# A two-layer diffusion trunk on one core: the norm of the second token block moves into the FFN's block, beside the first halves of six products

## The chip, the core and the metric

One core of a Trainium2 chip runs the whole program in one launch. The metric is the device time in microseconds. Engines by their names in the profile: PE (TensorE), DVE (VectorE), ACT (ScalarE), POOL (GpSimd), SP (SyncE, which here issues all the DMAs of the part in question).

## What is computed

Two layers work on 128 context tokens and 1024 latent tokens (1152 in all, 1024 features, fp32). The part around the change is the second half of each layer:

```
x = x + g1 * (y @ w_out)                       # y: output of the mixer
h = rms(x, norm_w[l, 1]) * (1 + sc2) + sh2     # mean square over the 1024 features of a token
u = dwconv(h @ w_up, conv_w, conv_b)           # 5632 columns, taps of 3 over the tokens
x = x + g2 * ((silu(a) * b) @ w_down)          # a, b: the halves of u
```

A product of fp32 quality is three matmuls on values split into a high and a low part (`split_matmul`, L89 to L91).

## The kernel before

Everything is kept transposed: features on the 128 partitions, tokens along the free axis, so x is the tile `x_t` of 8 rows of 1152 tokens. `P` is 128, `KT` 8, `KH` 4, `HALF` 576 tokens, `SIDE` and `SUB` 288. A *token block* b is the b-th quarter of each half of the tokens: 288 tokens of the left half and 288 of the right ("sides"). Each scope is a `Block` in which every engine has a program of its own; engines meet at its end. Semaphores order the work inside.

**`out_norm`** computes 16 output tiles v = 0 to 15 (`OUT_TILES`): 8 feature rows for token block 0, then the same 8 for block 1. For a tile PE does 2 sides x 8 rows x 3 matmuls of 288 columns. DVE adds the result to `x_t` (`add`, L634), ACT and DVE split the weights two tiles ahead into high and low (`split_w`, L495 and L625), ACT squares the new row (`square`, L505), and DVE adds the square to the running sum (`pile`, L644). PE waits for the low weights of tile v and for the add of tile v - 3. After 8 rows PE sums over the partitions with a matrix of ones (`total`, L590), and ACT takes ln and exp (`root`, L510, L513), which gives the inverse root mean square. Then come four norm steps q for the block, each of two feature rows (q and q + 4): DVE scales (`scale`, L653), ACT applies gain and shift (`shift`, L521), DVE forms four differences (`differences`, L661 to L666), and seven operands are split into high (ACT, L532 and L537) and low (DVE, L671 and L679) in `acts`. These are the seven activation operands of a Strassen form: the tokens' halves and the features' halves are the 2 x 2 blocks.

The steps of token block 0 run beside the tiles v = 8 to 15, placed by the dicts `begun`, `turned_in` and `ended` (a step every two tiles, from v = 8). Those of block 1 (q = 4 to 7) run after the last tile, in a loop at the end of the ACT and DVE programs. SP spills x to DRAM (`spill`, L463): block 0 after `load_w(11)`, block 1 at the end, and waits for both.

**`strassen_ffn`** then does the FFN. It has 22 steps t over pairs of weight tiles, each of 7 products i of 2 x 4 x 3 matmuls of 288 columns (168 a step). POOL forms four sums of weight quarters (L912, L913, L915, L919; the third of them makes product 1's operand), ACT makes `w_hi` (L938), DVE `w_lo` (L1049), PE multiplies, and ACT (`copy_m1`, L944) and DVE (`recombine`, L1068) read the seven results. On DVE the low part of the next step's operand i stands between the reads: lo(t+1, 0), read 0, lo(t+1, 1), read 1, lo(t+1, 2), and so on. The results use four pairs of PSUM banks in turn. The memory of `x_t` is reused (`take`): for `u`, `conv`, `m1`, the sums, the last quarter of the odd steps' weights and the taps `cw`. Step 0's weights are loaded in `out_norm` already (`ahead`). Ahead of its first instruction ACT, like DVE, waits for `cw`.

Of the kernel before, what the change touches and what calls it, by code (L numbers as in the profile page):

```python
# [377 lines left out]
def out_norm(nc, tag, l, d, x_t, y_tok, ident, x_from, x_to, ones, eps, mods, gains, acts, raw, w_first, ahead):  # L378
# [7 lines left out]
    with Scope(nc, tag) as s:  # L386
# [7 lines left out]
        x_in, spilled = [s.sem(f"x_in{k}") for k in range(KT)], s.sem("spilled")  # L394
# [53 lines left out]
        begun = {KT: 0, KT + 2: 1, KT + 4: 2, KT + 6: 3}  # L448
        turned_in = {KT + 1: 0, KT + 3: 1, KT + 5: 2, KT + 7: 3}
        ended = {KT + 2: 0, KT + 4: 1, KT + 6: 2, KT + 7: 3}  # L450

        with nc.Block() as block:
            @block.sync
            def _(sp):
# [25 lines left out]
                spill(1)  # L480
                sp.wait_ge(spilled, 16 * 2 * KT)
# [6 lines left out]
            def _(act):  # L488
# [72 lines left out]
                root(1)  # L561
                shift(KH)
                for q in range(KH, N_STEPS):
                    high_plain(q)
                    if q + 1 < N_STEPS:
                        shift(q + 1)
                    high_diff(q)

            @block.tensor
            def _(pe):  # L570
# [45 lines left out]
                pe.wait_ge(inverted, 1)  # L616
                total(1)

            @block.vector
            def _(dve):  # L620
# [17 lines left out]
                def pile(v_):  # L638
                    b, k = divmod(v_, KT)
                    if k:  # L640
                        dve.wait_ge(squared, v_ + 1)
                        if k >= 2:
                            dve.wait_ge(piled, (KT - 1) * b + k - 1)
                        dve.tensor_tensor(inv[:, b, :], inv[:, b, :], sq[:, k % 2, :], ALU.add).then_inc(piled, 1)  # L644
# [51 lines left out]
                for v_ in range(OUT_TILES):  # L696
# [3 lines left out]
                    if v_ in ended and v_ not in turned_in:  # L700
                        low_diff(ended[v_])
# [3 lines left out]
                    if v_ in ended and v_ in turned_in:  # L705
                        low_diff(ended[v_])
                    if v_ in begun:
                        scale(begun[v_])
                scale(KH)
                for q in range(KH, N_STEPS):  # L710
                    differences(q)
                    if q + 1 < N_STEPS:
                        scale(q + 1)
                    low_plain(q)
                    low_diff(q)


G_SLOTS = 4

# [24 lines left out]
def strassen_ffn(nc, tag, l, d, x_t, mods, acts, raw, arrived, x_from, x_to):  # L744
# [5 lines left out]
    with Scope(nc, tag) as s:  # L750
        odd = s.sb("raw_odd", [P, 3, QW])
        w_hi, w_lo = s.sb("w_hi", [P, ACTS, QW], F32R), s.sb("w_lo", [P, ACTS, QW], F32R)
        ps = s.bank_pairs(4)
        cw_in = s.sem("cw_in")
        odd_in = [s.sem("odd_in0"), s.sem("odd_in1")]
# [18 lines left out]
        sums = [take(QW) for _ in range(4)]  # L774
        odd_last = take(QW)
        cw = take(FT * 2 * 4).rearrange("p (t h n) -> p t h n", h=2, n=4)
# [9 lines left out]
        def source(t, i):  # L786
            return sums[SUM_OF[i]] if i in SUM_OF else quarter(t, *RAW_OF[i])
# [4 lines left out]
        def halves(t, i):  # L792
            return pair_of(t, i)[:, :, 0:SUB]

# [34 lines left out]
        with nc.Block() as block:  # L829
            @block.sync  # L830
            def _(sp):
                sp.dma_start(cw, d["ffn_conv"][l]).then_inc(cw_in, 16)
# [48 lines left out]
                for n, (b, f, j, _) in enumerate(steps):  # L881
# [5 lines left out]
                    if n % FT == 10:  # L887
                        sp.wait_ge(g_stored, 16 * FT)
# [13 lines left out]
            def _(pool):  # L902
                Scope.clear_ended(pool)
                for t in range(FT):
                    (a1, a2), (b1, b2) = [[quarter(t, half, part) for part in range(2)] for half in range(2)]
                    for half in range(2):
# [2219 lines left out]
```

## Time and profile before

| | us |
|---|---|
| median of 3 runs | 3456.2 (3452.51 to 3477.64) |
| the profiled execution | 3463.67 |
| its span, first to last instruction | 3461.6 |
| PE busy | 3231.2 (93%) |
| DVE busy | 1865.5 (54%) |
| ACT busy | 1415.6 (41%) |
| POOL busy | 460.2 (13%) |
| granted clock of PE, mean | 0.958 |

All times of rows are of the profiled execution, in us from the span's start. Layer 0's `out_norm` ends and its FFN begins at about 910 us, layer 1's at about 2680 us. A row's start and duration can overlap the next row's by a pipeline's depth.

### The profile page before, as it was taken

What the parts mean: (1) busy time and instruction counts of PE and PEld (TensorE: products, weight loads), DVE (VectorE), ACT (ScalarE), POOL (GpSimd) and SP (SyncE); (2) the same over time, 40 slices, a digit from 0 to 9 for tenths busy, and PEclk for the clock granted to TensorE, in tenths of its full rate; (3) what the DMA queues carried; (4) which work ended last, traced back from release to release, by engine and by line L of the source; (5) the groups of instructions that cost most, each with busy time, mean ns of one, the idle gap of its engine ahead of it and who ended that gap; (6) DMA issues with size and microseconds to landing.
All of it is one profiled execution on the core that took longest, in us unless ns stands there. A gap on an engine that the chain in (4) does not pass through costs nothing. (4 is left out here: it accounts for less than half of the span.)

```text
span 3461.6 us, 57673 instructions
## 1 busy us (share of the span) xinstructions
PE 3231.2 (93%) x23164; PEld 2961.8 (86%) x23164; DVE 1865.5 (54%) x3213; ACT 1415.6 (41%) x2415; POOL 460.2 (13%) x370
## 2 busy tenths in 40 slices
PE   5999988889599999999799999999985999999998
PEld 3998755669599999999588997877775999999998
DVE  4321265455777777533523102677657777777432
ACT  4354115774533333422426213455546333333322
POOL 0000361000122222000000001111100322220000
PEclk7999999999799999999899998999988999999999
DMA  5115541014222221544634314222132222223643
GB/s 221 43 71 184 181 149 41 2 42 139 66 77 77 77 76 55 193 151 145 255 133 159 122 53 149 93 69 100 31 131 89 73 77 77 77 77 103 212 158 120
DMA packets 157512, 376.11 MB, mean 109 GB/s; under 512 B 23552, under 2 KB 92672, under 8 KB 149312
## 3 DMA queue, kind: packets, MB, share of 16 engines
q1 hardware_dynamic: 142176, 345.29, 29.3%
q0 software_dynamic: 4704, 17.70, 1.4%
q10 hardware_dynamic: 10368, 9.44, 0.8%
q8 instruction: 185, 3.03, 0.4%
q14 instruction: 79, 0.65, 0.1%
HBM read 292.03 MB, written 80.35 MB: 108 GB/s over the span
## 5 line engine op out<-in xcount | busy, mean ns | idle before, releaser
L89 PE MATMUL ffn__pair<-hf__acts,ffn__w_hi 128*128 128x288 f32 x2464 | 726.5, 295 | 66.7 <-DVE ffn__w_lo L1049 66.7
L91 PE MATMUL ffn__pair<-hf__acts,ffn__w_hi 128*128 128x288 f32 x2464 | 728.6, 296 | 0.0
L90 PE MATMUL ffn__pair<-hf__acts,ffn__w_lo 128*128 128x288 f32 x2464 | 727.0, 295 | 0.0
L89 PEld LDWEIGHTS ffn__pair<-hf__acts,ffn__w_hi 128*128 128x128 f32 x2464 | 463.8, 188 | 68.3 <-DVE ffn__w_lo L1049 68.3
L90 PEld LDWEIGHTS ffn__pair<-hf__acts,ffn__w_lo 128*128 128x128 f32 x2464 | 463.7, 188 | 0.0
L91 PEld LDWEIGHTS ffn__pair<-hf__acts,ffn__w_hi 128*128 128x128 f32 x2464 | 463.6, 188 | 0.0
L89 PE MATMUL ffn__pair<-hf__acts 128*128 128x384 f32 x1056 | 352.9, 334 | 2.9 <-issue 2.9
L91 PE MATMUL ffn__pair<-hf__acts 128*128 128x384 f32 x1056 | 352.7, 334 | 0.0
L90 PE MATMUL ffn__pair<-hf__acts 128*128 128x384 f32 x1056 | 352.7, 334 | 0.0
L1082 DVE SCALAR_TENSOR_TENSOR all__x_t<-all__x_t 128x127 f32<-128x127 f32 x352 | 271.1, 811 | 29.4 <-ACT all__x_t L951 29.3
L938 ACT ACTIVATE ffn__w_hi<-all__x_t 128x512 fp32r<-128x512 f32 x198 | 125.5, 635 | 380.3 <-PE ffn__pair L91 363.6
L1068 DVE TENSOR_TENSOR all__x_t<-ffn__pair,all__x_t 128x576 f32<-128x576 f32 x308 | 228.2, 753 | 87.5 <-PE ffn__pair L91 82.0
L89 PEld LDWEIGHTS ffn__pair<-hf__acts 128*128 128x128 f32 x1056 | 198.2, 188 | 3.3 <-issue 3.3
L90 PEld LDWEIGHTS ffn__pair<-hf__acts 128*128 128x128 f32 x1056 | 198.2, 188 | 0.0
L91 PEld LDWEIGHTS ffn__pair<-hf__acts 128*128 128x128 f32 x1056 | 198.2, 188 | 0.0
L1096 DVE TENSOR_TENSOR hf__acts<-all__raw,hf__acts 128x1024 fp32r<-128x1024 f32 x100 | 122.4, 1224 | 132.2 <-ACT hf__acts L966 132.0
L2869 DVE COPY_PREDICATED lin__att<-lin__mask,lin__pair 128x384 f32<-128x384 int16 x168 | 118.5, 705 | 113.2 <-PE lin__pair L2764 100.9
L2764 PEld LDWEIGHTS lin__pair<-lin__qz,lin__f 64*128 64x128 f32 x2016 | 142.1, 195 | 38.7 <-issue 35.0
L972 ACT ACTIVATE hf__acts<-ffn__raw_odd 128x384 fp32r<-128x384 f32 x132 | 68.4, 518 | 240.9 <-PE ffn__pair L91 217.9
L2764 PE MATMUL lin__pair<-lin__qz,lin__f 64*128 64x64 f32 x2016 | 165.4, 286 | 1.0 <-DVE lin__att L2869 1.0
L89 PE MATMUL out__bank<-hf__acts 128*128 128x288 f32 x512 | 153.5, 300 | 9.5 <-DVE hf__acts L625 8.6
L1049 DVE TENSOR_TENSOR ffn__w_lo<-all__x_t,ffn__w_hi 128x512 fp32r<-128x512 f32 x198 | 155.5, 786 | 8.7 <-ACT ffn__w_hi L938 8.7
(355 smaller groups left out, 6911.1 us busy)
## 6 DMA issues: line engine op xcount, KB each, us to landing
all__raw<-w_down SPq DMA_DIRECT2D x100, 512.0 KB, 3.7
ffn_g<-all__x_t SPq DMA_DIRECT2D x44, 576.0 KB, 3.2
ffn__raw_odd<-ffn_g SPq DMA_DIRECT2D x132, 192.0 KB, 3.7
all__raw<-w_up SPq DMA_DIRECT2D x44, 512.0 KB, 4.7
in__ada_w<-w_ada SPq DMA_DIRECT2D x16, 1024.0 KB, 5.2
n1a__ada_w<-w_ada SPq DMA_DIRECT2D x16, 1024.0 KB, 8.5
out__w_raw<-w_out SPq DMA_DIRECT2D x28, 512.0 KB, 3.6
all__raw<-w_t SPq DMA_DIRECT2D x27, 512.0 KB, 4.3
```

The lines of the kernel that those rows point to most:

```text
L89: pe.matmul(out, w_hi, v_lo, start=first, stop=False)
L90: pe.matmul(out, w_lo, v_hi, start=False, stop=False)
L91: return pe.matmul(out, w_hi, v_hi, start=False, stop=last)
L938: act.activation(w_hi[:, i, :], source(t, i), ACT.Copy).then_inc(hi_done, 1)
L972: act.activation(g_hi(n), g_raw(n), ACT.Copy).then_inc(g_hi_done, 1)
L1049: dve.tensor_tensor(w_lo[:, i, :], source(t, i), w_hi[:, i, :].bitcast(F32), ALU.subtract)\
L1068: dve.tensor_tensor(split2(out), halves(t, PRODUCT_OF[r]), split2(kept), ALU.add)\
L1082: dve.scalar_tensor_tensor(conv[half][:, o[0]:o[1]], u[half][:, i[0]:i[1]], cw[:, t, half, 2 * right:2 * right + 1], conv[half][:, o[0]:o[1]],
L1096: dve.tensor_tensor(lo, dn_raw(j), hi.bitcast(F32), ALU.subtract).then_inc(dn_lo_done, 1)
L2764: last = pe.matmul(scores[m % 2][:, h, c * half:(c + 1) * half], f[rows_of(h), n % 3, 2 + j, c * P:(c + 1) * P], qz[rows_of(h), n % 2, j, ...
L2869: dve.copy_predicated(out[:, :, :, late:late + size], msk.to_broadcast([P, 2, late_cols // size, size]), scores[m % 2][:, :, 0:late_cols]. ...
```

## The change

In `out_norm` the norm steps of token block 0 are placed closer (two steps in three tiles), and those of block 1, with PE's last `total`, the last `root` and `spill(1)`, are taken out. The last `pile` writes its sum into row 0 of block 0 of `x_t`, which has been spilled by then.

```diff
-        begun = {KT: 0, KT + 2: 1, KT + 4: 2, KT + 6: 3}
-        turned_in = {KT + 1: 0, KT + 3: 1, KT + 5: 2, KT + 7: 3}
-        ended = {KT + 2: 0, KT + 4: 1, KT + 6: 2, KT + 7: 3}
+        begun = {KT: 0, KT + 1: 1, KT + 3: 2, KT + 4: 3}
+        turned_in = {KT + 1: 0, KT + 2: 1, KT + 4: 2, KT + 5: 3}
+        ended = {KT + 2: 0, KT + 3: 1, KT + 5: 2, KT + 6: 3}
...
-                spill(1)
-                sp.wait_ge(spilled, 16 * 2 * KT)
...
+                        if v_ == OUT_TILES - 1:
+                            dve.wait_ge(spilled, 16 * KT)
+                            dve.wait_ge(scaled, 2 * KH)
+                            out = both(x_t[:, 0, :], 0)
```

In `strassen_ffn` the norm's work buffers lie in block 0 of `x_t`, and step 0 keeps its sums outside it (`sum_at`: in `odd` and in the place of one weight quarter). What reuses `x_t` waits for `room_free`: all 28 low parts of the norm and both spills. Weights of step 1 wait for step 0's low parts, because `odd` holds step 0's sums.

```diff
+FIRST_BANKS = ((0, 6), (1, 7), (2, 0), (3, 6), (4, 1), (5, 7), (2, 0))
+FREED_WITH = (5, 6, 6, 6, 0, 0, 0)
...
+        def room_free(eng):
+
+            eng.wait_ge(n_lo_done, ACTS * KH)
+            eng.wait_ge(spilled, 16 * 2 * KT)
+
+        def sum_at(t, n):
+            if t:
+                return later_sums[n]
+            return quarter(0, 1, 0) if n == 2 else odd[:, (0, 1, None, 2)[n], :]
...
+                for k in range(KT):
+                    into = x_from[:, k, :].rearrange("p (a n) -> p a n", a=2)[:, :, SIDE:2 * SIDE]
+                    sp.dma_start(into, both(k, 1)).then_inc(spilled, 16)
...
+                    else:
+                        sp.wait_ge(lo_done, ACTS)
...
+                            if t == 1 and part:
+                                room_free(sp)
...
+                    if t == 1:
+                        room_free(pool)
                     pool.tensor_tensor(sums[0], b1, b2, ALU.add).then_inc(summed, 1)
+                    if t == 0:
+                        pool.wait_ge(summed, 1)
...
-                act.wait_ge(cw_in, 16)
...
-                for i in range(ACTS - 1):
+                for i in range(3):
                     hi_up(0, i)
+                root()
+                hi_up(0, 3)
+                shift(0)
+                for q in range(KH):
+                    high_plain(q)
+                    if q + 1 < KH:
+                        shift(q + 1)
+                    high_diff(q)
+                    if q < 3:
+                        hi_up(0, 4 + q)
```

`copy_m1` and `recombine` of step 0 wait for `room_free` and read each side with an instruction of its own. `cw` has memory of its own, and its wait stands at its first use. PE begins with the `total` of block 1, does the first sides (block 0) of products 0 to 5, then the second sides of products 0 and 1 row by row as the norm delivers them, then the rest:

```diff
+                for i in range(6):
+                    pe.wait_ge(lo_done, i + 1)
+                    for k in range(KH):
+                        first_half(i, 0, k)
+                pe.wait_ge(n_logged, 2)
+                for k in range(KH):
+                    pe.wait_ge(n_lo_done, ACTS * (k + 1))
+                    for i in range(2):
+                        op = first_half(i, 1, k)
+                        if k == KH - 1:
+                            op.then_inc(mm, 1)
+                for i in range(2, 6):
+                    if i < 4:
+                        pe.wait_ge(m1_copied, 1)
+                    else:
+                        pe.wait_ge(recombined, LAST_READ[1])
+                    for k in range(KH):
+                        op = first_half(i, 1, k)
+                    op.then_inc(mm, 1)
+                pe.wait_ge(lo_done, 7)
+                pe.wait_ge(recombined, LAST_READ[2])
+                for side in range(2):
+                    for k in range(KH):
+                        op = first_half(6, side, k)
+                op.then_inc(mm, 1)
+                for t in range(1, FT):
...
-                for i in range(ACTS - 1):
+                for i in range(3):
                     lo_up(0, i)
+                scale(0)
+                lo_up(0, 3)
+                for q in range(KH):
+                    differences(q)
+                    if q + 1 < KH:
+                        scale(q + 1)
+                    low_norm(q)
+                    if q < 3:
+                        lo_up(0, 4 + q)
```

Products 0 to 3 of step 1 wait for later reads of step 0 than before, since the banks of step 0 are laid out otherwise: product 0 for the sixth read (`FREED_WITH[0]` is 5, `LAST_READ[5]` is 6), products 1 to 3 for the seventh. `root`, `shift`, `scale`, `differences` and the splits are the same instructions as in `out_norm`, for latent tokens alone. The same change holds in both layers.

## Rows read from the trace of the kernel before

**Rows 1.** Busy time by stretch: PE, PEld, DVE, ACT, POOL, clock, DMA share, GB/s

```profile
840.00:860.00 20.00, 20.00 (x154) 20.00 (x154) 17.07 (x33) 13.99 (x27) 0.00 (x0) 1.00 0.26 79
880.00:900.00 20.00, 1.47 (x4) 0.50 (x2) 16.04 (x38) 15.66 (x31) 0.00 (x0) 0.50 0.24 83
900.00:920.00 20.00, 5.54 (x26) 5.54 (x27) 13.61 (x29) 9.62 (x21) 5.47 (x4) 0.52 0.19 58
```

**Rows 2.** Waits in both layers' seams: engine, line, releaser, total us, times, longest

```profile
PE ffn__pair L89 <- DVE ffn__w_lo L1049: 33.0, 1, 33.0
...
PE ffn__pair L89 <- DVE ffn__w_lo L1049: 33.7, 1, 33.7
```

**Rows 3.** Timeline of PE, layer 0, then layer 1: start us, us, instruction

```profile
879.22 2.26 PE L590 MATMUL out__bank<-out__inv,all__ones 128*128 128x288 f32 x4 [3.15 <-DVE out__inv L644]
...
914.46 0.61 PE L89 MATMUL ffn__pair<-hf__acts,ffn__w_hi 128*128 128x288 f32 x1 [32.98 <-DVE ffn__w_lo L1049]
...
2684.29 0.61 PE L89 MATMUL ffn__pair<-hf__acts,ffn__w_hi 128*128 128x288 f32 x1 [33.68 <-DVE ffn__w_lo L1049]
```

**Rows 4.** Timeline of DVE, last output tiles of layer 0

```profile
853.79 1.23 DVE L625 TENSOR_TENSOR hf__acts<-out__w_raw,hf__acts 128x1024 fp32r<-128x1024 f32 x1 [1.68 <-ACT hf__acts L495]
...
876.18 0.94 DVE L634 SCALAR_TENSOR_TENSOR all__x_t<-out__bank,all__mods,all__x_t 128x288 f32<-128x288 f32 x2
...
878.31 0.76 DVE L644 TENSOR_TENSOR out__inv<-out__inv,out__sq 128x576 f32<-128x576 f32 x1 [1.19 <-ACT out__sq L505]
...
881.69 1.55 DVE L679 TENSOR_TENSOR hf__acts<-out__diff,hf__acts 128x288 fp32r<-128x288 f32 x4
```

**Rows 5.** Waits, 780 to 1000 us: DVE for ACT's weight split

```profile
DVE hf__acts L625 <- ACT hf__acts L495: 5.0, 3, 1.7
```

**Rows 6.** Timeline of ACT: the root of the second block, layer 0

```profile
881.16 1.28 ACT L510 ACT_TABLE_LOAD   x1
...
884.66 0.68 ACT L513 ACTIVATE out__inv<-out__inv 128x576 f32<-128x576 f32 x1
```

**Rows 7.** Timeline of DVE: norm of the second block, layer 0

```profile
887.82 0.46 DVE L661 TENSOR_TENSOR out__diff<-out__v 128x288 f32<-128x288 f32 x1 [1.02 <-ACT out__v L521]
...
893.87 0.46 DVE L661 TENSOR_TENSOR out__diff<-out__v 128x288 f32<-128x288 f32 x1
...
908.68 1.55 DVE L679 TENSOR_TENSOR hf__acts<-out__diff,hf__acts 128x288 fp32r<-128x288 f32 x4
```

**Rows 8.** Timelines of SP, ACT, POOL: start of the FFN block, layer 0

```profile
910.51 0.34 SPq L832 DMA_DIRECT2D all__x_t<-ffn_conv  x1
...
912.39 0.63 ACT L938 ACTIVATE ffn__w_hi<-all__raw 128x512 fp32r<-128x512 f32 x1 [4.26 <-DMA all__x_t<-ffn_conv]
...
912.59 1.26 POOL L912 TENSOR_TENSOR all__x_t<-all__raw 128x512 f32<-128x512 f32 x1 [350.36 <-issue]
...
916.81 0.63 ACT L938 ACTIVATE ffn__w_hi<-all__x_t 128x512 fp32r<-128x512 f32 x1 [3.79 <-POOL all__x_t L915]
...
917.35 0.61 ACT L938 ACTIVATE ffn__w_hi<-all__raw 128x512 fp32r<-128x512 f32 x1
```

**Rows 9.** Timelines of DVE and POOL: FFN steps 0 and 1, layer 1

```profile
2688.45 0.68 DVE L1049 TENSOR_TENSOR ffn__w_lo<-all__raw,ffn__w_hi 128x512 fp32r<-128x512 f32 x1
...
2690.56 1.53 POOL L912 TENSOR_TENSOR all__x_t<-ffn__raw_odd,all__x_t 128x512 f32<-128x512 f32 x1 [2.58 <-DVE ffn__w_lo L1049]
...
2693.75 1.74 POOL L915 TENSOR_TENSOR all__x_t<-all__x_t,ffn__raw_odd 128x512 f32<-128x512 f32 x1
...
2696.20 1.28 DVE L1049 TENSOR_TENSOR ffn__w_lo<-all__x_t,ffn__w_hi 128x512 fp32r<-128x512 f32 x1 [1.19 <-ACT ffn__w_hi L938]
```

**Rows 10.** DMA issues, 910 to 918 us: KB each, us to landing

```profile
all__x_t<-w_up SPq DMA_DIRECT2D x1, 256.0 KB, 4.4
```

**Rows 11.** Timeline of ACT, both layers: copy after the first product of step 1

```profile
942.32 0.65 ACT L944 ACTIVATE all__x_t<-ffn__pair 128x576 f32<-128x576 f32 x1 [2.49 <-PE ffn__pair L91]
...
2711.38 0.65 ACT L944 ACTIVATE all__x_t<-ffn__pair 128x576 f32<-128x576 f32 x1 [2.48 <-PE ffn__pair L91]
```

More of the change, by code:

```diff
@@ L375, with out_norm @@
 N_STEPS = 2 * KH
[L378 removed]
+def out_norm(nc, tag, l, d, x_t, y_tok, ident, x_from, x_to, ones, eps, mods, gains, acts, raw, w_first, spilled, ahead):
     by_token = y_tok is not None
@@ L699, in _ @@
                     pile(v_)
-                    if v_ in ended and v_ not in turned_in:
+                    if v_ in ended:
                         low_diff(ended[v_])
@@ L773, in strassen_ffn, with both, h, diff @@
         m1, u2, u3 = take(HALF), take(HALF), take(HALF)
-        sums = [take(QW) for _ in range(4)]
+        later_sums = [take(QW) for _ in range(4)]
         odd_last = take(QW)
-        cw = take(FT * 2 * 4).rearrange("p (t h n) -> p t h n", h=2, n=4)
+        def both(row, b):
+            return x_t[:, row, :].rearrange("p (a n) -> p a n", a=2)[:, :, b * SIDE:(b + 1) * SIDE]
+        inv = both(0, 0)
+        def h(q, half):
+            return both(1 + 2 * (q % 2) + half, 0)
+        def diff(n):
+            return both(5 + n // 2, 0)[:, n % 2, :]
+        def plain(q, i):
+            half, side = {Q11: (0, 0), Q21: (1, 0), Q22: (1, 1)}[i]
+            return h(q, half)[:, side, :]
+        def home(q, i, low):
+            return acts[:, i, low, q, SIDE:2 * SIDE]
+        def room_free(eng):
[5 more added lines that the diff above has]
+            return quarter(0, 1, 0) if n == 2 else odd[:, (0, 1, None, 2)[n], :]
         def quarter(t, half, part):
@@ L786, in source @@
         def source(t, i):
-            return sums[SUM_OF[i]] if i in SUM_OF else quarter(t, *RAW_OF[i])
+            return sum_at(t, SUM_OF[i]) if i in SUM_OF else quarter(t, *RAW_OF[i])
         def pair_of(t, i):
@@ L905, in _ @@
                     (a1, a2), (b1, b2) = [[quarter(t, half, part) for part in range(2)] for half in range(2)]
+                    sums = [sum_at(t, n) for n in range(4)]
                     for half in range(2):
@@ L972, in hi_down, with root, shift, high_plain @@
                     act.activation(g_hi(n), g_raw(n), ACT.Copy).then_inc(g_hi_done, 1)
-                for i in range(ACTS - 1):
-                    hi_up(0, i)
+                def root():
+                    act.wait_ge(n_summed, 1)
+                    for side in range(2):
+                        act.activation(inv[:, side, :], ps[3][:, side, 0:SUB], ACT.Ln, bias=eps[:, 0:1], scale=1.0 / D)\
+                            .then_inc(n_logged, 1)
+                    act.wait_ge(n_logged, 2)
+                    act.activation(inv, inv, ACT.Exp, scale=-0.5).then_inc(n_inverted, 1)
+                def shift(q):
+                    for half in range(2):
+                        k = q + KH * half
+                        act.wait_ge(n_scaled, 2 * q + half + 1)
+                        act.activation(h(q, half), h(q, half), ACT.Identity, bias=mod(mods, l, SH2, k, 1),
+                                       scale=gains[:, l, 1, k, 1:2]).then_inc(n_shifted, 1)
+                def high_plain(q):
+                    act.wait_ge(n_shifted, 2 * q + 2)
+                    for i in (Q11, Q21, Q22):
+                        act.activation(home(q, i, 0), plain(q, i), ACT.Copy).then_inc(n_hi_done, 1)
+                def high_diff(q):
+                    for n, i in enumerate((T1, T3, T2, T4)):
+                        act.wait_ge(n_diffed, 4 * q + n + 1)
+                        act.activation(home(q, i, 0), diff(n), ACT.Copy).then_inc(n_hi_done, 1)
+                for i in range(3):
+                    hi_up(0, i)
+                root()
[8 more added lines that the diff above has]
+                        hi_up(0, 4 + q)
                 for t in range(FT):
-                    hi_up(t, 6)
+                    if t:
+                        hi_up(t, 6)
                     copy_m1(t)
```

113 lines of the change are left out of this document (77 added, 36 removed).

## The prediction

> **What bounds the kernel now.** I read the page first: PE is busy in 93% of the span, so only stretches where PE stands still, or runs at the lower clock, can give time back. The busy time by stretch shows them: from 840 to 860 us PE works without a gap (154 matmuls in 20 us, 0.130 us each), from 880 to 900 only four matmuls run and the clock is at 0.50, and from 900 to 920 26 run at 0.52 [rows 1]. The waits name the gap: in each layer PE waits once for the first `w_lo` of the FFN, 33.0 and 33.7 us [rows 2]. So there are two seams, one a layer; I work one out on layer 0. PE ends the last product of `out_norm` at 876.07 (the `total` starts at 879.22 after 3.15 us of idle time), and starts the first FFN matmul at 914.46 [rows 3]. Two seams of 38.4 us hold 77 us, 2.2% of the time. That is the most that could be had, and the question is how far it shrinks.
>
> Inside the seam DVE sets the pace: it goes from one operation to the next through the four norm steps (first difference at 887.82, last low part ends at 908.68 + 1.55 = 910.23 [rows 7]), with ACT beside it. Then come 4.2 us of block change, the wait of ACT for `cw` (issued at 910.51, ACT starts at 912.39 [rows 8]) and one split. After that PE has 168 matmuls for step 0. The mark I carry through is the end of the first product of step 1, which ACT's copy follows at once: 942.3 in layer 0, 2711.4 in layer 1 [rows 11]. From there on PE is continuous before, and I find nothing in the change that touches it later. PE's own sum agrees: 914.46 + 192 x 0.1315 = 939.7 (0.1315 is the spacing of neighbouring rows), 2.2 us for the low clock at the start (26 matmuls took 5.5 us in place of 3.4 [rows 1]), and the pipeline's depth.
>
> **The change, step by step, in layer 0.** The tail of the old chain is shortened by overlap, but three pieces ahead of it get longer.
>
> *Closer steps in `out_norm`.* Before, DVE ends its work on token block 0 and the last tile at 881.69 + 1.55 = 883.24, and the last `pile` ended at 878.31 + 0.76 = 879.07, with eleven operations of step 3 behind it [rows 4]. A tile takes PE 48 x 0.1315 = 6.3 us. DVE needs for a tile 0.94 (add) + 1.2 (split) + 0.75 (pile) = 2.9 us [rows 4] and for a norm step some 6.0 us (the period of the steps in the seam [rows 7], the same operations). One step in two tiles is 5.9 us a tile, just under 6.3. Two steps in three tiles is 6.9, over it. So DVE falls behind from tile 9 on. Now all of step 3 stands ahead of the last `pile`, so by the sum of the work that one ends at 883.24 at the earliest with the old gaps. There is one more gap: after each `scale` ACT's shift stands ahead of its weight split, and DVE waits for it, 1.68 us, three times before, 5.0 us in all [rows 5], four times now, less some overlap at the end. I take 1.5 us: the block ends at 884.7, 5.6 us later than the old `pile`. On the way the low weights of tiles 13 to 15 come late, and PE stands about 3.6 us there. Bounds: no slip (0), and 7.5 us.
>
> *The way to the inverse.* Before, the `total` followed the `pile` and the exp ended at 884.66 + 0.68 = 885.34, 6.3 us after the `pile` [rows 6]. Now ACT does `hi_up(0, 1)` and `hi_up(0, 2)` first, and the first of them waits for POOL's third sum. From the block's end to POOL's first sum: 912.59 - 910.23 = 2.4 us; to ACT's second split, released by that third sum, 916.81 - 912.59 = 4.2 us; the two splits 1.1 us [rows 8]; then the root, 4.2 us from the table load on [rows 6]. Together 11.8 us, 5.5 more than before. The inverse is ready at 896.5. Nothing covers this: DVE has only three weight splits to do meanwhile. The new order inside POOL (second sum behind the first) adds under 0.1.
>
> *The norm itself.* Before 910.23 - 885.34 = 24.9 us [rows 6, 7]. In it now stand `lo_up(0, 4)`, (0, 5), (0, 6), 0.6 us each in a queue that has no gap (0.68 less the overlap with the next [rows 9]); `lo_up(0, 3)` falls into the 1.0 us in which DVE waited for the first shift [rows 7]. So 26.7 us, and the last low part ends at 923.2 = N, 13 us later than before. ACT's four extra splits fit into its pauses. The spill now runs beside this and is long done; before it was hidden too.
>
> *The tail.* Before: 942.3 - 910.23 = 32.1 us. After N PE has left 6 + 48 + 24 = 78 matmuls of step 0, 10.3 us, in place of 22.1. But step 1's first product has to wait for the sixth read of step 0, and that stands in DVE's queue behind `lo_up(1, 1)`, which waits for POOL's third sum of step 1, which waits for `room_free` and for the last quarter of its weights. That quarter's DMA is issued only at N. Its landing took 4.4 us beside three other loads [rows 10]; the small `cw` 1.9 us [rows 8]; I take 3.0 for 256 KB alone. Three sums of POOL: 2693.75 + 1.74 - 2690.56 = 4.9 us beside DVE's splits, three times 1.26 = 3.8 alone [rows 8, 9]; I take 4.4. ACT's split 0.65. Then on DVE `lo_up(1, 1)` 0.7 to 1.3 [rows 9], five reads at 0.85 (two instructions of 288 columns; an `add` of that size takes 0.94 [rows 4]), three more splits at 0.6: 7.1 us with the splits. Sum 3.0 + 4.4 + 0.65 + 7.1 + waits 0.4 = 15.6 us. PE itself could be there at N + 0.9 + 0.9 (copy of `m1`) + the rest of the 78 + 2.2 for the clock, about N + 14, so DVE decides. The product takes 3.3 us more: N + 18.9 = 942.1. Bounds for the tail: 2.4 us less (everything uncontended), 4.7 more.
>
> The Trainium skill, SBUF — State Buffer, Who interferes with whom, says that a DVE instruction with two SBUF inputs contends with a GpSimd instruction that reads SBUF, while one with at most one SBUF input does not. Rows 9 fit the first half. By the second half the reads, which take one input from PSUM, would leave POOL alone, the three sums would take 3.8 us, and each seam would be 0.6 us shorter than I say.
>
> **Sum.** Layer 0: 942.1 against 942.3, -0.2 us. Layer 1 repeats layer 0 with an offset of 1769.83 (2684.29 against 914.46 [rows 3]), but its clock rose earlier and its mark stood 0.8 us earlier in that frame, so there it is +0.6 us. Together +0.4 on the profiled execution's 3463.67 (its span is 3461.6, and it lies 7.5 above the median of 3456.2). Carried to the median: 3456.5 us. In parts, a seam: + 5.6 + 5.5 + 1.8 - 13.2.
>
> **Rivals.** *Slip absent, faster.* DVE keeps up in `out_norm`, because its gaps close instead of opening. For it: DVE has 1.7 us gaps there [rows 5]. Against: those gaps are waits for ACT, and they recur with each step. Price 5.6 a seam: 3445 us. *Nothing given back, faster.* The steps come in time and the root is not delayed either: 12 to 13 us a seam, 3431 us. Against: the chain of program orders above; it needs two things not to happen. *The clock, slower.* PE works in short bursts during the norm, and the granted clock was 0.50 to 0.52 around the gap [rows 1], the lower of the two levels (1.2 GHz); it rose only within the continuous run behind it. In the new tail PE has pauses (the copy of `m1`, the second read, the sixth read). If it stayed low there, 78 matmuls at 0.24 us each (288 columns at 1.2 GHz) take 18.7 us, plus 1.8 of waits: PE is at N + 20.5 and not at 15.6, and the next product runs low too, + 2.6. That is +7.5 a seam: 3471 us, slower than before. It decides once more than some 30 of the 78 run low. Against: before it rose within about 20 matmuls. The Trainium skill, TensorE: Matmul & The Clock Gate, The HAM clock gate, says "the default state is throttled, and activity releases the throttle"; by that the bursts would not help, and only the run after N would, which is this rival's first half. That the first sides are not done early at all can be left out: they wait for weights alone, and the last of those, `lo_up(0, 5)`, stands behind the second norm step.
>
> **How the numbers follow.** Forecast (a wash, within 4 us) 0.6; slip absent 0.17; nothing given back 0.05; clock 0.18. The bounds of the parts are -8 and +8 a seam, so -16 and +16. The median of few runs moves by some us as well (3452.5 to 3477.6 before). Range 3441 to 3471. One per cent, about what a measurement of this kernel can tell from no change, is 34.6 us: no rival reaches it. Faster by more: 0.02; within: 0.95; slower: 0.03, for a wait that I have not seen.
>
> **What would show it.** Right: `pile` of tile 15 ends 5 to 6 us later; PE waits for `w_lo` in tiles 13 to 15; exp ends 11 to 12 us behind it; the last low part of the norm near 923; the sixth read sets the start of step 1 near N + 15.6; copy of `m1` of step 1 at about 942 and 2712. Wrong: a continuous PE through tile 15, a clock at 0.5 beyond N + 6, or a gap of PE in steps 1 to 3.

## The result: 60 us longer in its first four executions, outside the place of the change

The changed kernel took 3526.2 us (median of 4 executions, 3523.4 to 3529.6), the kernel before 3466.2 (4 executions, 3452.5 to 3477.6; three of them are the three of the table above). That is 60 us more, and 70 more than the forecast of 3456.5, whose range went up to 3471. The ratio is 1.0175, 95% interval 1.0127 to 1.0223. Ratios leave out executions that are over 1.5% above the fastest of the same kernel, called long below, but here all four of the changed kernel are long by the measure of its later sets, so none was left out.

The page of the changed kernel, its profiled execution (3529.56 us):

```profile
span 3527.8 us, 57691 instructions
...
PE 3324.6 (94%) x23164; PEld 3033.8 (86%) x23164; DVE 1860.6 (53%) x3227; ACT 1417.3 (40%) x2417; POOL 460.2 (13%) x370
...
PEclk8999989999899999999899995589989899999999
```

PE has the same 23164 matmuls, and 93.4 us more of busy time than the 3231.2 before. The granted clock has two digits of 5 in a row. A digit is a fortieth of the span, 88 us: these two are 2117 to 2293 us. The change acts at two places, near 890 and near 2720 us, and neither is there. The row of the kernel before has an 8 and a 9 in that place:

```profile
PEclk7999999999799999999899998999988999999999
```

The busy time by stretch says it with numbers. It is the linear scans of layer 1, code that the change doesn't touch (PE busy and its matmuls, clock, DMA share, GB/s; PE's rows alone). Before, then after:

```profile
2150.00:2200.00 50.00, 50.00 (x490) 1.00 0.26 94
2200.00:2250.00 50.00, 49.76 (x483) 1.00 0.32 112
2250.00:2300.00 50.00, 49.63 (x467) 1.00 0.19 62
```

```profile
2150.00:2200.00 50.00, 50.00 (x272) 0.50 0.18 64
2200.00:2250.00 50.00, 50.00 (x269) 0.50 0.09 32
2250.00:2300.00 50.00, 50.00 (x270) 0.50 0.17 58
2300.00:2350.00 50.00, 49.76 (x394) 0.83 0.24 83
```

PE is busy in 49.6 us or more of every 50 in both, and issues little more than half as many matmuls in the second. Single rows of PE's timeline in that stage show why, first before, then after:

```profile
2144.82 0.50 PE L2721 MATMUL lin__bank<-lin__spans,lin__g_hi 128*128 128x512 f32 x1
2145.16 0.39 PE L2722 MATMUL lin__bank<-lin__spans,lin__g_lo 128*128 128x512 f32 x1
2145.49 0.89 PE L2764 MATMUL lin__pair<-lin__qz,lin__f 64*128 64x64 f32 x12
```

```profile
2143.21 0.79 PE L2878 MATMUL lin__bank<-lin__spans,lin__g_hi 128*128 128x512 f32 x1
2143.80 0.63 PE L2879 MATMUL lin__bank<-lin__spans,lin__g_lo 128*128 128x512 f32 x1
...
2145.84 1.55 PE L2921 MATMUL lin__pair<-lin__qz,lin__f 64*128 64x64 f32 x12
```

At full clock (2.4 GHz) twelve small matmuls take 0.89 us, at the lower level (1.2 GHz) 1.55. In the profile before, PE was at the lower level for 17.1 us from 2127.5 on, and rose at 2144.6. In the profile after it was there from 2129.7 on, for 187.7 us. Until the one rises the two executions run 2.3 to 2.4 us apart, matmul by matmul. These are the longest stretches near the start of the scans; each profile has others too, in the first 11 us and at the end of the scans (36.9 us before, 6.0 after). All together PE spends 65.6 us of the scans at the lower level before and 205.2 after. Below, *the low stretch* is the longest one near the start.

So the extra time splits as follows, each part from PE's timelines. *Out* is the first product of `out_norm` (the row `out__bank<-hf__acts`), *down* the first matmul of the FFN's down product (its first row with 384 columns).

| us | before | after | difference |
|---|---|---|---|
| up to *out*, layer 0 | 767.1 | 772.8 | +5.7 |
| *out* to *down*, layer 0 (the change) | 640.81 | 638.96 | -1.85 |
| first to last matmul of layer 1's scans | 416.3 | 480.8 | +64.5 |
| *out* to *down*, layer 1 (the change) | 638.89 | 637.72 | -1.17 |

The 5.7 us arise before anything of the change has run; PE's time at the lower level there is 88.7 us before and 95.6 after. The rest of the program agrees within 1.5 us. Rows of the four marks, before and after:

```profile
767.12 0.38 PE L89 MATMUL out__bank<-hf__acts 128*128 128x288 f32 x1
...
1407.93 0.41 PE L89 MATMUL ffn__pair<-hf__acts 128*128 128x384 f32 x1 [1.38 <-issue]
```

```profile
772.83 0.38 PE L89 MATMUL out__bank<-hf__acts 128*128 128x288 f32 x1
...
1411.79 0.41 PE L89 MATMUL ffn__pair<-hf__acts 128*128 128x384 f32 x1 [1.39 <-issue]
```

### The profile page after: what moved, and what is told of

It is laid out like the page before. It is cut to its first block and busy times, and to the rows that moved or that the text cites. A ratio compares the mean times of both kernels' runs of the same rounds, so it can differ in the third digit from the quotient of the medians.

```text
span 3527.8 us, 57691 instructions
## 1 busy us (share of the span) xinstructions
PE 3324.6 (94%) x23164; PEld 3033.8 (86%) x23164; DVE 1860.6 (53%) x3227; ACT 1417.3 (40%) x2417; POOL 460.2 (13%) x370
## 5 line engine op out<-in xcount | busy, mean ns | idle before, releaser
L89 PE MATMUL ffn__pair<-hf__acts,ffn__w_hi 128*128 128x288 f32 x2464 | 735.6, 299 | 33.5 <-DVE ffn__w_lo L1160 23.4
L91 PE MATMUL ffn__pair<-hf__acts,ffn__w_hi 128*128 128x288 f32 x2464 | 734.6, 298 | 0.0
L89 PEld LDWEIGHTS ffn__pair<-hf__acts,ffn__w_hi 128*128 128x128 f32 x2464 | 469.8, 191 | 37.7 <-DVE ffn__w_lo L1160 26.6
L91 PEld LDWEIGHTS ffn__pair<-hf__acts,ffn__w_hi 128*128 128x128 f32 x2464 | 469.8, 191 | 0.0
L1202 DVE SCALAR_TENSOR_TENSOR all__x_t<-all__x_t,ffn__cw 128x127 f32<-128x127 f32 x352 | 271.2, 812 | 28.3 <-ACT all__x_t L994 28.1
L1182 DVE TENSOR_TENSOR all__x_t<-ffn__pair,all__x_t 128x576 f32<-128x576 f32 x294 | 217.9, 753 | 79.1 <-PE ffn__pair L91 73.8
L2921 PEld LDWEIGHTS lin__pair<-lin__qz,lin__f 64*128 64x128 f32 x2016 | 167.8, 226 | 45.7 <-issue 42.4
L2921 PE MATMUL lin__pair<-lin__qz,lin__f 64*128 64x64 f32 x2016 | 193.1, 319 | 1.0 <-DVE lin__att L3026 1.0
L1009 ACT ACTIVATE hf__acts<-all__raw 128x1024 fp32r<-128x1024 f32 x100 | 105.5, 1055 | 131.9 <-PE ffn__pair L91 68.3
```

Of the source, the lines that this page charges most:

```text
L89: pe.matmul(out, w_hi, v_lo, start=first, stop=False)
L91: return pe.matmul(out, w_hi, v_hi, start=False, stop=last)
L1009: act.activation(dn_home(home)[0], dn_raw(j), ACT.Copy).then_inc(dn_hi_done, 1)
L1182: op = dve.tensor_tensor(split2(out), halves(t, PRODUCT_OF[r]), split2(kept), ALU.add)
L1202: dve.scalar_tensor_tensor(conv[half][:, o[0]:o[1]], u[half][:, i[0]:i[1]], cw[:, t, half, 2 * right:2 * right + 1], conv[half][:, o[0]:o[1]],
L2921: last = pe.matmul(scores[m % 2][:, h, c * half:(c + 1) * half], f[rows_of(h), n % 3, 2 + j, c * P:(c + 1) * P], qz[rows_of(h), n % 2, j, ...
```

## The seam in the profile after

Where the change acts, the profile has the steps of the prediction. PE's and DVE's waits from 780 to 1000 us (total, times, longest), which answer to [rows 2] and [rows 5]:

```profile
PE ffn__pair L89 <- DVE ffn__w_lo L1160: 11.7, 3, 5.0
PE ffn__pair L89 <- DVE hf__acts L1255: 4.7, 2, 3.8
PE ffn__pair L1121 <- PEq L452: 3.4, 1, 3.4
PE out__bank L89 <- DVE hf__acts L614: 3.1, 4, 1.9
PE ffn__pair L89 <- DVE all__x_t L1185: 0.5, 1, 0.5
```

```profile
DVE hf__acts L614 <- ACT hf__acts L493: 6.7, 4, 1.7
```

The wait of 33.0 us and that of 3.15 for the `pile` have become eleven of 23.4 in all, and four of them (3.1 us) stand in the last four tiles of `out_norm`, where before there was none. Less idle time isn't the gain, though: from *out* to the copy behind the first product of step 1 (the mark) PE is busy for 10.9 us more (149.6 for 138.7) with as many matmuls, since they now run in many short bursts, 98 of them at the lower level in place of 24, and the mark comes only 1.9 us sooner. DVE's wait for ACT's weight split comes four times in place of three. The end of the last `pile`, the root, the last low part of the norm, and the copy behind the first product of step 1, which answer to [rows 4, 6, 7, 11]:

```profile
889.81 0.76 DVE L638 TENSOR_TENSOR all__x_t<-out__inv,out__sq 128x576 f32<-128x576 f32 x1 [0.75 <-ACT out__sq L503]
...
925.71 2.66 DVE L1255 TENSOR_TENSOR hf__acts<-all__x_t,hf__acts 128x288 fp32r<-128x288 f32 x7
```

```profile
896.74 0.63 ACT L974 ACTIVATE ffn__w_hi<-ffn__raw_odd 128x512 fp32r<-128x512 f32 x1 [5.25 <-POOL ffn__raw_odd L953]
897.28 0.61 ACT L974 ACTIVATE ffn__w_hi<-all__raw 128x512 fp32r<-128x512 f32 x1
897.91 1.28 ACT L1020 ACT_TABLE_LOAD   x1
...
901.41 0.69 ACT L1023 ACTIVATE all__x_t<-all__x_t 128x576 f32<-128x576 f32 x1
...
946.17 0.65 ACT L980 ACTIVATE all__x_t<-ffn__pair 128x576 f32<-128x576 f32 x1 [3.18 <-PE ffn__pair L91]
```

To compare them, take off the 5.7 us by which this execution is late. ACT's splits for products 1 and 2 stand ahead of the root, the first after 5.25 us of waiting for POOL's sum. The clock in the seam is not 0.50 as in [rows 1]:

```profile
880.00:900.00 20.00, 13.17 (x67) 12.16 (x66) 11.42 (x24) 6.85 (x12) 5.05 (x4) 0.77 0.36 124
900.00:920.00 20.00, 11.72 (x54) 11.14 (x54) 16.83 (x37) 14.29 (x30) 0.00 (x0) 0.76 0.00 0
920.00:940.00 20.00, 15.27 (x85) 14.46 (x84) 13.70 (x31) 10.28 (x22) 5.38 (x4) 0.79 0.35 110
```

As predicted, the first product of step 1 waits for the sixth read, if only by 0.45 us:

```profile
942.71 0.37 PE L89 MATMUL ffn__pair<-hf__acts,ffn__w_hi 128*128 128x288 f32 x1 [0.45 <-DVE all__x_t L1185]
```

## Experiments

Two theories. The first: the scans' clock is not the change's doing. As recorded for the first runs it said that the change moves the scans in time against the steps of the clock; in the later runs it says only that the low stretch differs from one execution to the next in every kernel. The second, the rival: something that the change does brings the long stretch. The seams are read in the same profiles. Three sets of runs were made, each on a chip of its own with the kernel before beside them (19, 29 and 29 executions).

### One layer alone

The change in layer 1 alone (l1_only) and in layer 0 alone (l0_only), the other layer with the functions of the kernel before.

```diff
-                out_norm(...)
-                strassen_ffn(...)
+                if l in (1,):        # l0_only: (0,)
+                    out_norm(...)
+                    strassen_ffn(...)
+                else:
+                    out_norm_before(...)
+                    strassen_ffn_before(...)
```

> The change in layer 1 alone; layer 0 as before. Theory 1 (the seams gain 1 to 2 us each, and the rest is the clock of PE in layer 1's linear scans, whose lower level lasted 17 us before and 188 us after, because the change moved the scans against the steps of the clock): the program is the one of before up to the scans, so they take what they take before, and the total is 1 us below before, within 15 us. Theory 2 (something that the changed program holds, its memory, semaphores or place in the code, slows the scans whatever their time): about 3526 us here too. Theory 3 (the change's new code in layer 1 costs the time in its own place): some 30 to 65 us over before.

> The change in layer 0 alone; layer 1 as before. Theory 1 (clock steps in the scans): layer 1's scans start where they did after the whole change, so the lower level lasts about 188 us there again and the total is about 3527 us. Theory 2 (content of the program): about 3526 or, if the content is layer 1's, 3456. Theory 3 (cost in layer 1's own place): 3454 to 3466 us.

l1_only: 3449.3 us median (3442.1 to 3476.3, 10 executions), ratio 0.9976 (0.9942 to 1.001). l0_only: 3453.4 (3446.6 to 3522.5, 10 executions), ratio 1.0015 (0.9993 to 1.0037). One execution of l0_only took 3522.5, like the changed kernel's first four, and nine did not. What counts more: of the kernel before, six of 19 in this set took 3500.5 to 3532.9. The long executions need no change at all. The first theory in its recorded form is refuted as well: it had layer 0's change alone bring 188 us at the lower level and 3527 us again, by moving the scans. They start at 2114.17 us in l0_only, at 2114.81 in the changed kernel's first profile and at 2114.64 in a later one (after_again), and the low stretch lasts 34.1, 187.7 and 3.4 us. When the scans start doesn't decide it.

The seams are clean. With its own layer changed a seam is 638.97 (layer 0) and 637.98 (layer 1); left as before it is 640.81 and 639.00 (before_gap2 and b_warm below have 640.95 and 640.77, and 640.23 and 639.44). Each layer has its gain alone, whatever the other does.

### The scans started later

A small block ahead of layer 1's scans holds the changed kernel up: DVE clears 64 columns (a_gap0), or 64 and then twice 760 (a_gap2, and before_gap2 on the kernel before).

```diff
+                    with Scope(nc, "gap") as gs:
+                        waited = gs.sem("waited")
+                        with nc.Block() as block:
+                            @block.vector
+                            def _(dve):
+                                for r, n in enumerate((64,) + (760,) * 2):
+                                    dve.memset(x_t[:, r, 0:n], 0.0).then_inc(waited, 1)
+                                dve.wait_ge(waited, 3)
```

> The whole change, and ahead of layer 1's linear scans a block of its own with one short memset on DVE. It moves the scans by the time of a block change, some 2 to 4 us. Theory 1: the scans meet the steps of the clock in another place, so the lower level may last anything between 15 and 190 us; any value under 100 us speaks for it. Theory 2: 170 us or more at the lower level, as after the change.

> As a_gap0, with two more memsets of 760 columns, so the scans start some 1.7 us later than there. Theory 1: the time at the lower level differs from a_gap0's in at least one of the two kernels and needn't be near 188 us. Theory 2: 170 us or more at the lower level in both.

> The kernel before with a small block ahead of the scans in which DVE clears 64 and then twice 760 columns (about 2 us later start). The same delay on the changed kernel gave 3521 and 167 us at the lower clock. Theory 1: anything from 3450 to 3535, by the stretch of lower clock that the profile shows at the scans. Theory 2 (the changed content matters): under 3465 with a stretch under 50 us.

a_gap0: 3476.4 us, scans 425.3 us from first to last matmul, low stretch 44.4. a_gap2: 3521.2, scans 471.7, low stretch 167.3. before_gap2: 3478.3, scans 421.2, low stretch 34.1. Each is one execution. Taken alone, the pair a_gap2 and before_gap2 would speak for the rival; with a quarter of the executions of every kernel long, it says little. The delay doesn't cure it or bring it on by a rule that I could name.

### The changed kernel again, twice

No edit.

> The changed kernel as it is, to learn how its executions spread. Theory 1 (the time at the lower clock in layer 1's scans is a matter of the single execution; the seams gain 3 us): it spreads like the kernel before, which took 3442 to 3533 us in 19 executions, six of them over 3500, so several of its executions are under 3480. Theory 2 (the changed program holds the scans back, and neither half of the change alone does): all executions at 3520 to 3530.

> The changed kernel as it is, a third time, paired with the two others of this call. Theory 1: ratio to before 0.995 to 1.005, seams 638.9 and 637.8, first to last matmul of the scans anything from 398 to 481 us. Theory 2: over 3500 in most executions. Where the profile of this run shows a short low stretch at the scans it is near 3445, where a long one near 3520.

On the second chip: 3447.8 us median (3445.3 to 3474.2, 12 executions), none long, ratio 0.998 (0.9955 to 1.0006). On the third: 3451.9 (3447.2 to 3525.2, 12 executions), three long (3517.4, 3521.3, 3525.2), ratio 0.9984 (0.9955 to 1.0012). Both profiled executions have a low stretch of 3.4 us at the scans, and the scans take 398.5 and 404.5 us. The stage by stretch in the profile of after_third, to be held against that of the same kernel above:

```profile
2100.00:2150.00 50.00, 41.04 (x301) 0.83 0.66 234
2150.00:2200.00 50.00, 50.00 (x494) 1.00 0.15 50
2200.00:2250.00 50.00, 49.76 (x477) 1.00 0.34 116
```

The same instructions, 494 matmuls in 50 us or 272. Its seams are 639.00 and 637.72, those of after_again 638.88 and 638.02.

Over all sets the kernel before has 22 of 81 executions over 3500 us, the changed kernel 7 of 28: 27% and 25%. Without the first four of each it is 22 of 77 and 3 of 24. No long execution of the kernel before was profiled, but each execution's mean clock is on record: 0.937 to 0.948 in its 22 executions over 3500 us, 0.952 to 0.968 in the others of the same sets, and 0.941 to 0.944 in the seven of the changed kernel. Of the 14 profiles three are of long executions (after, a_gap2, root_timed), with low stretches of 167 to 188 us, and the other eleven have 51 us or less. The rival falls: nothing here shows that the change makes long executions more frequent, and it doesn't make them all long. That the first four of the changed kernel were all long, and the four of before beside them all short, is not explained by these shares if executions are independent (0.27 to the fourth is 0.5%). What ties the four together stays open, and so the first 60 us are traced to the clock in the scans, but not to what set it.

### Root ahead of the later weight splits

The term of 5.5 us in the sum: ACT takes the root behind the first split in place of the third, DVE `scale(0)` likewise. The kernel is the same in root_first (one execution) and root_timed (12).

```diff
-                for i in range(3):
-                    hi_up(0, i)
+                hi_up(0, 0)
                 root()
-                hi_up(0, 3)
+                for i in range(1, 4):
+                    hi_up(0, i)
...
-                for i in range(3):
-                    lo_up(0, i)
+                lo_up(0, 0)
                 scale(0)
-                lo_up(0, 3)
+                for i in range(1, 4):
+                    lo_up(0, i)
```

> The changed kernel, with the root of the second block and its first scale ahead of the splits of products 1 and 2, which wait for POOL. My prediction's sum has 5.5 us a seam for that order. If it is on the chain, the stretch from the first matmul of the output product to the first of the down product falls from 639.0 to about 633.5 us in layer 0 and from 637.8 to about 632.5 in layer 1. If something else is late next (the weight splits of product 3, the first halves on PE), it falls by under 2 us. The total is not asked here.

> The same kernel as in the run with one look (root and scale(0) ahead of the later weight splits of step 0), now timed. Each seam was 3.7 to 4.0 us shorter there than in the changed kernel, which itself is 1.0 to 1.9 us shorter than before. If seams add up in the time, this kernel is 10 to 11 us under before: a ratio near 0.997. Theory 1 (the scans' clock differs by execution, in every kernel alike): some executions may lie at 3500 or more, as before has them in 14 of 48, and the median tells little about 10 us. Theory 2 (the changed content brings the long low stretch): most executions over 3480.

ACT's timeline in root_timed, whose last `pile` ends at 888.82 + 0.76 = 889.58:

```profile
889.88 0.63 ACT L974 ACTIVATE ffn__w_hi<-all__raw 128x512 fp32r<-128x512 f32 x1 [1.09 <-PEq L452]
890.53 1.28 ACT L1020 ACT_TABLE_LOAD   x1
...
894.40 0.68 ACT L1023 ACTIVATE all__x_t<-all__x_t 128x576 f32<-128x576 f32 x1
```

The inverse is there 5.5 us behind the `pile`, 6.0 sooner than in the changed kernel. DVE's last low part ends at 920.92 + 2.66 = 923.58, 34.0 us behind the `pile` in place of 37.8: the splits that were moved now stand inside the norm and take 2.2 us of it back. The seams are 635.16 (both profiles), and 634.06 and 634.24: 3.5 to 4.0 us shorter than those of after_again and after_third, where 5.3 to 5.5 was expected. The order of ACT and DVE is on the chain, as the prediction had it.

In the time it doesn't show. Timed, five of 12 executions were over 3500 (3507.7 to 3517.5), and the ratio of the others is 0.9999 (0.9965 to 1.0033), with a fastest one of 3433.7 against 3442.6 of before. The two profiles of this one kernel make the cleanest pair: a low stretch of 51.2 us and 428.3 us for the scans in root_first (3463.4 us), 167.3 and 472.9 in root_timed (3515.0). The scans differ by 44.6 us of the 51.6 between the two executions. With all their time at the lower level counted (87.8 and 187.0 us), that is 0.45 us for each further us there. Root_timed by stretch:

```profile
2150.00:2200.00 50.00, 50.00 (x268) 0.50 0.10 37
2200.00:2250.00 50.00, 50.00 (x272) 0.50 0.08 26
2250.00:2300.00 50.00, 50.00 (x275) 0.50 0.16 58
```

### Extra matmuls at the start of the scans

Wide matmuls (384 columns) are put between the first small ones, into banks that the next product overwrites: nothing else of the program reads them. In the kernel before (b_warm), the changed kernel (a_warm), and the changed kernel with the root first (warm_root).

```diff
+                def keep_busy(out, count):
+                    for _ in range(count):
+                        pe.matmul(out, g_hi[:, 0, 0:P], g_hi[:, 0, 0:UW], start=True, stop=True)
...
+                    if n < 2:
+                        keep_busy(bank[:, 0:UW], 3)
...
+                    if n < 1:
+                        keep_busy(scores[m % 2][:, 0, 0:UW], 4)
```

> The kernel before, with extra matmuls at the start of layer 1's linear scans, whose results are overwritten: three of 384 columns ahead of each piece of the first two units and four ahead of each score of the first unit. They keep PE at work while it would wait for DVE and ACT. Theory 1: the clock rises with them and stays up, so executions gather within 10 us, at 3440 to 3450, and none is over 3480. If the long stretches at the lower level had another cause than the little work that PE has at the start, executions over 3500 remain.

> The changed kernel with the same extra matmuls at the start of the scans. Theory 1: it gathers as b_warm does, and 3 us below it (1.85 in layer 0's seam, 1.0 in layer 1's), so at 3437 to 3447. Theory 2: 3500 us or more remains in most executions, or at least 30 us over b_warm.

> The changed kernel with both: root first, and extra matmuls into banks that are overwritten at the start of the linear scans (their results are not used). Runs with the extra matmuls had no execution over 3469 in 24, against 14 of 48 of before over 3500. Theory 1: no execution over 3480 again, seams 635.2 and 634.1, scans 405 to 411 us, a median near 3448 (3455.6 of the changed kernel with extra matmuls, less 7.7). If an execution over 3500 comes, the extra matmuls do not keep the clock up and the 24 were luck.

b_warm: 3463.1 us median (3451.4 to 3469.0), ratio 1.0004 (0.9982 to 1.0025). a_warm: 3455.6 (3447.2 to 3461.1), 0.9989 (0.9973 to 1.0006). warm_root: 3449.1 (3438.6 to 3456.1), 0.9975 (0.9948 to 1.0003). Twelve executions each, and none of the 36 over 3469, where of the kernels without the extra matmuls about every fourth is over 3500. In the three profiles the scans' first 3 to 5 us are at the lower level, and from 2122 us to their last 32 us there is none. Warm_root by stretch:

```profile
2100.00:2150.00 50.00, 42.48 (x303) 0.93 0.54 192
2150.00:2200.00 50.00, 50.00 (x493) 1.00 0.27 95
```

Two expectations were missed: b_warm was to lie at 3440 to 3450 within 10 us, and a_warm at 3437 to 3447. Both are 10 us and more higher, and b_warm spreads over 18. The price is 6 to 13 us against the best case: the scans take 404.8 to 411.2 us in place of 398.4, and on the one chip that timed both, a_warm's median is 7.9 us above that of the changed kernel without the extra matmuls (3447.8). So a short execution loses by them and a long one is avoided.

Without the long executions the change can be timed. On the same chip a_warm's mean is 3455.7 and b_warm's 3461.5, 5.8 us apart, a ratio of 0.9983 with 0.9974 to 0.9992 as the 95% interval of a resampling of 12 and 12 executions. It is the one timed comparison whose interval leaves out 1. The seams of the two profiles account for 3.6 of it (1.75 and 1.81); the scans also differ, by 6.5 us, where b_warm has one more stretch of 13.7 us at the lower level near their end, and that is not the change's place. By medians warm_root is 3449.1 against 3459.5 of before in the same set; its ratio among short executions has an interval that still touches 1. Over all executions its mean is 3448.3 against 3477.9, a ratio of 0.9915, with 0.988 to 0.995 as the 95% interval of a resampling of the 12 and 29 executions. Its slowest execution is 3456.1, where those of before and of the changed kernel in the same set are 3535.1 and 3525.2; the mean of the latter is 3468.1. On the chip of a_warm, where none of the changed kernel's 12 executions was long, the extra matmuls bring its mean nothing (3455.7 for 3452.7).

The same subtraction gives the root's worth once more: warm_root's seams are 635.05 and 633.88, a_warm's 639.02 and 637.63.

## Why the prediction was wrong, and where it was right

**The step that failed is the carry from the seam to the time.** The sum was worked out for two seams, and "Carried to the median: 3456.5 us" then took the other 3385 us as fixed, with "some us" for the median of few runs. What the runs showed in its place is the clock in layer 1's scans: 64.5 us of the 66.2 between the two profiled spans, while the seams gained 1.85 and 1.17. I had the clock as a rival inside the seam only. The row of PE's clock in the page before already showed digits below 9 outside it, among them one of 8 at the scans, and I didn't ask what they were worth or whether they would come again. The bound "no rival reaches" 34.6 us was for that reason false: one stretch of the clock elsewhere was worth 64.5 us. Three executions with a spread of 25 us were too few to show that a quarter lie above 3500. The 0.03 for slower should have been several times that, and the range should have had a second part near 3525. Against that, the changed kernel's later medians, 3447.8 and 3451.9, lie in the range and 5 to 9 us under the forecast.

**The seam, term by term** (layer 0; from the rows after, less the 5.7 us):

| term | said | measured |
|---|---|---|
| last `pile` later | +5.6 | 890.57 - 5.71 - 879.07 = 5.8 |
| `pile` to inverse | 11.8 | 902.10 - 890.57 = 11.5 |
| inverse to last low part N | 26.7 | 928.37 - 902.10 = 26.3 |
| N to the mark | 18.9 | 946.17 - 928.37 = 17.8 |
| mark against before | -0.2 | 946.17 - 5.71 - 942.32 = -1.9 |
| layer 1 against before | +0.6 | -1.2 |

- *Closer steps.* Right in size and cause: four gaps of up to 1.7 us in place of three, and PE stands 3.1 us in the last four tiles, for 3.6 said in the last three. The rival "slip absent" falls.
- *Way to the inverse.* Right; root_timed, with the inverse 6.0 us sooner, confirms that the order of ACT's queue is its cause. Of the 5.5 us, only 3.5 to 4.0 can be had by changing the order, since the splits have to be done somewhere.
- *The tail* is 1.1 us too long in the sum. The last quarter's DMA took 2.6 us (issued at 928.40, POOL starts at 931.04), for 3.0 said, though two more loads were issued at 928.83. POOL's three sums took 4.1 for 4.4, and a read of two sides 0.81 for 0.85:

```profile
931.04 1.60 POOL L948 TENSOR_TENSOR all__x_t<-ffn__raw_odd,all__x_t 128x512 f32<-128x512 f32 x1 [32.98 <-DMA all__x_t<-w_up]
932.61 1.27 POOL L951 TENSOR_TENSOR all__x_t<-ffn__raw_odd 128x512 f32<-128x512 f32 x1
933.84 1.27 POOL L953 TENSOR_TENSOR all__x_t<-all__x_t,ffn__raw_odd 128x512 f32<-128x512 f32 x1
```

  The first began beside DVE's split (930.82 to 931.51) and took 0.33 us more than the two others; DVE's read from PSUM (931.43 to 932.24) ran beside it as well, so this row alone can't tell the two apart. Rows of the kernel before can: two sums, at 935.03 and 936.28, ran beside a read alone for 0.36 and 0.41 us of their time, and each took 1.29:

```profile
935.03 1.29 POOL L912 TENSOR_TENSOR all__x_t<-all__raw 128x512 f32<-128x512 f32 x1 [7.94 <-DVE ffn__w_lo L1049]
936.28 1.29 POOL L913 TENSOR_TENSOR all__x_t<-all__raw 128x512 f32<-128x512 f32 x1
```

```profile
935.96 0.76 DVE L1068 TENSOR_TENSOR all__x_t<-ffn__pair,all__x_t 128x576 f32<-128x576 f32 x1 [1.16 <-PE ffn__pair L91]
936.69 1.43 DVE L1049 TENSOR_TENSOR ffn__w_lo<-all__x_t,ffn__w_hi 128x512 fp32r<-128x512 f32 x1
```

  The last row shows the other side: where the sum began first, it is DVE's split that takes longer, 1.43 us for 0.68. The Trainium skill, SBUF — State Buffer, Who interferes with whom, says that a DVE instruction with two SBUF inputs contends with a GpSimd instruction that reads SBUF, and one with at most one SBUF input does not. The traces agree with both halves. The prediction's 4.4 us for the three sums held 0.6 of contention; measured, it was 0.3.
- *Clock in the seam.* The rival falls, by a narrow margin. By stretch the clock is 0.76 to 0.79 in place of 0.50 and 0.52. But its sign of being wrong, "a clock at 0.5 beyond N + 6", came in layer 0: PE was at the lower level until N + 6.7 us in this profile and N + 6.5 in after_again (N + 5.5 in after_third), and 25, 25 and 21 of the 78 matmuls ran there, where some 30 would have made PE the later one. PE was ready 0.5 to 1.0 us ahead of the sixth read. In layer 1 the 0.8 us of lead that I gave the kernel before came out at 0.7 (-1.17 for -1.85).
- *Nothing given back* falls with the three terms above.

So the change is worth 3 us of 3460 between the marks, 0.1%. Some of it is lost again outside them: from *down* in layer 1 to the last instruction takes 284.98 to 285.02 us in every profile in which layer 1 is changed and 284.41 to 284.45 in every other, 0.55 us more for a reason that stays open. In the measured terms a seam of layer 0 is + 5.8 (slip) + 5.2 (11.5 for 6.3) + 1.4 (26.3 for 24.9) - 14.3 (17.8 for 32.1) = -1.9. What the overlap wins in the tail is given back ahead of it, by DVE behind in the closer steps, by the root behind POOL's sums and by the splits inside the norm. That the gain is real is shown by the seams of every profile and, in the time, by a_warm against b_warm; the ratios of the two later sets, 0.998 and 0.9984, have intervals that hold 1 and can't show it.

## What to carry to other kernels

Before forecasting a small change, read the clock row outside the place of the change and price it: here one stage cost up to 82 us more by the clock alone (480.8 against 398.3 for the scans), over twenty times what the change was worth. With a spread of 0.7% in three executions, take more executions of the kernel before and look at all their times, not at the median. Judge a change of some us by the distance between two marks around it in each profile, and check the same distance in several profiles of both kernels. In layer 0 it repeated within 0.2 us from chip to chip (640.77 to 640.95 before, 638.88 to 639.08 changed), while the whole time moved by 90. In layer 1 it did so within 0.5 us for the changed kernel (637.63 to 638.09), but spread over 1.3 us where the seam was as before (638.89 to 640.23), since the clock rose between 7.2 and 10.3 us behind the norm there.

## What was not expected of the hardware

- PE stayed at the lower level for up to 188 us while its records are busy in all of it (50.00 of 50.00 us, 272 matmuls), and in other executions of the same instructions that stretch lasted 3.4 us. In the first pair of profiles the two executions came to the stage 2.4 us apart and with the same spacing, and one rose where the other did not. The Trainium skill, TensorE: Matmul & The Clock Gate, The HAM clock gate, says that activity releases the throttle. In these rows an unbroken run of busy records, most of them matmuls of 64 partitions by 64 columns, went on for 188 us without a rise. With wide matmuls between the first ones, none of 36 executions was long. Whether their width or their number does it, or only the delay that they bring, wasn't tried apart; a delay alone (the gap runs) left a stretch of 34 to 167 us in each of three executions.
- Why one execution falls into the long stretch and the next doesn't is open.
